# Rotary embedding of the retention heads: by a copy within SBUF and GpSimd, instead of by TensorE and VectorE

## What is computed

```python
def rotary(x, pos):
    ...
    x1, x2 = xf[..., :half], xf[..., half:]
    return jnp.concatenate([x1 * cos - x2 * sin, x2 * cos + x1 * sin], axis=-1)

def retention_mixer(cols, norm_w, pos):
    q, k, v, g = jnp.split(cols, 4, axis=-1)
    o = retention_chunkwise(rotary(q), rotary(k), v)     # scores * decay, times v
    mu = jnp.mean(o, axis=-1, keepdims=True)
    var = jnp.mean(jnp.square(o - mu), axis=-1, keepdims=True)
    o = (o - mu) * lax.rsqrt(var + NORM_EPS) * norm_w
    return jax.nn.silu(g) * o

def hybrid_layer(x, ...):
    proj = rms_norm(x, attn_norm_w) @ w_in
    mixed = jnp.concatenate([retention_mixer(ret_cols), dsa_mixer(dsa_cols), dilated_mixer(dil_cols)], axis=-1)
    x = x + mixed @ w_out
    h = rms_norm(x, mlp_norm_w)
    return x + jnp.square(jax.nn.relu(h @ w_up)) @ w_down
```

## Time and profile before

| | |
|---|---|
| time, median of 3 runs | 2440.71 us (2439.87 to 2441.47) |
| the profiled execution: its own time | 2440.98 us |
| its span in the profile | 2439.1 us |
| TensorE busy | 2382.6 us (98% of the span) |
| weight load of TensorE | 1905.6 us (78%) |
| VectorE busy | 1041.8 us (43%) |
| ScalarE busy | 955.3 us (39%) |
| GpSimd busy | 1026.4 us (42%) |

### The profile page before, as it was taken

One profiled execution on the slowest core, in us unless ns is written; L12 is line 12 of the kernel. 1 busy time (PEld: TensorE's weight loads), 2 busy tenths in 40 slices (PEclk: granted clock), 3 DMA queues, 4 the chain that ended last, 5 costly groups with the idle time before them and its releaser, 6 DMA issues.

```text
span 2439.1 us, 29458 instructions
## 1 busy us (share of the span) xinstructions
PE 2382.6 (98%) x11848; PEld 1905.6 (78%) x11848; DVE 1041.8 (43%) x1922; ACT 955.3 (39%) x1329; POOL 1026.4 (42%) x815
## 2 busy tenths in 40 slices
PE   8999999999999989999999989999999999999997
PEld 6777588888877767888888768888889769788887
DVE  4677641121337766211225545422224768322224
ACT  5344452232443445422335355421224485422223
POOL 4433144444444232444444453434444335444442
PEclk9999999999999999999999999999999999999999
DMA  4212123232232121323323212223323313322331
GB/s 162 79 52 96 34 88 104 88 103 87 83 108 86 36 95 35 104 87 103 104 87 117 87 35 70 83 90 104 104 85 106 104 37 102 104 87 87 104 104 52
DMA packets 138279, 212.36 MB, mean 87 GB/s; under 512 B 7456, under 2 KB 65952, under 8 KB 137888
## 3 DMA queue, kind: packets, MB, share of 16 engines
q1 hardware_dynamic: 138144, 210.48, 26.4%
HBM read 208.36 MB, written 2.10 MB: 86 GB/s over the span
## 4 chain that ended last, share of the span: by engine, by line
PE 54%; DVE 4%; ACT 4%; issue 1%; POOL 1%; ACTq 0%; DVEq 0%
PE ps L312 48%; PE ps L337 2%; POOL w_lo L275 1%; PE ps L1826 1%; DVE h_lo L569 1%; PE ps L845 1%; DVE x L692 1%; ACT w_hi L266 1%; PE ps L868 1%; PE ps L826 1%; DVE tmp_both L687 1%; ACT L493 0%; ACT h_hi L561 0%; PE ps L1298 0%; ACT r L1918 0%
## 5 line engine op out<-in xcount | busy, mean ns | idle before, releaser
L275 POOL TENSOR_TENSOR w_lo<-raw,w_hi 128x512 fp32r<-128x512 f32 (+1 forms) x776 | 992.7, 1312 | 1370.5 <-ACT w_hi L266 1370.2
L312 PE MATMUL ps<-h_hi,w_hi 128*128 128x512 f32 x1696 | 682.5, 402 | 14.2 <-POOL w_lo L275 13.8
L312 PE MATMUL ps<-h_hi,w_lo 128*128 128x512 f32 x1696 | 663.3, 391 | 0.0
L312 PE MATMUL ps<-h_lo,w_hi 128*128 128x512 f32 x1696 | 662.7, 391 | 0.0
L266 ACT ACTIVATE w_hi<-raw 128x2048 fp32r<-128x2048 f32 (+2 forms) x196 | 361.4, 1854 | 578.4 <-PE ps L312 457.6
L312 PE MATMUL ps<-hid_hi,w_hi 128*128 128x512 f32 x992 | 391.3, 394 | 4.8 <-DVE hid_lo L939 3.9
L312 PEld LDWEIGHTS ps<-h_hi,w_hi 128*128 128x128 f32 x1696 | 318.5, 188 | 98.0 <-issue 18.2
L312 PE MATMUL ps<-hid_hi,w_lo 128*128 128x512 f32 x992 | 388.1, 391 | 0.0
L312 PE MATMUL ps<-hid_lo,w_hi 128*128 128x512 f32 x992 | 387.9, 391 | 0.0
L312 PEld LDWEIGHTS ps<-h_lo,w_hi 128*128 128x128 f32 x1696 | 318.3, 188 | 69.9 <-issue 5.2
L312 PEld LDWEIGHTS ps<-h_hi,w_lo 128*128 128x128 f32 x1696 | 317.8, 187 | 70.4 <-issue 0.2
(11 more groups left out here) (304 smaller groups left out, 2775.6 us busy)
## 6 DMA issues: line engine op xcount, KB each, us to landing
raw<-in_w_up SPq DMA_DIRECT2D x32, 1024.0 KB, 5.5
raw<-in_w_down SPq DMA_DIRECT2D x32, 1024.0 KB, 5.0
raw<-in_ffn_w_gate SPq DMA_DIRECT2D x44, 512.0 KB, 3.9
raw<-in_ffn_w_up SPq DMA_DIRECT2D x44, 512.0 KB, 4.9
raw<-in_w_in SPq DMA_DIRECT2D x20, 1024.0 KB, 4.9
raw<-in_ffn_w_down SPq DMA_DIRECT2D x20, 1024.0 KB, 5.0
raw<-in_w_out SPq DMA_DIRECT2D x8, 1024.0 KB, 5.0
raw<-in_ev_w_in SPq DMA_DIRECT2D x8, 1024.0 KB, 5.3
```

Of the source, the lines that this page charges most:

```text
L275: pool.tensor_tensor(w_lo[slot.buf][:, k, 0:slot.width], raw[r][:, k, 0:slot.width], w_hi[slot.buf][:, k, 0:slot.width].bitcast(F32), ALU. ...
L312: mm = pe.matmul(o, lh, rh, start=first and q == 0, stop=last and q == 2, skip_group_check=True)
```

## The change

The matrix `rot_m` goes. SP copies the four blocks of `retqk` within SBUF with the halves of each head exchanged (8 transfers of 32 partitions by 4 KB, into the places of dilated queries that are no longer needed). POOL multiplies the copies with signed sines (4 instructions), after the next slot's low half multiplies q and k with the cosines (4) and adds (4), each 128x512. The tables of cosines and sines are loaded early, the decays alone later. With the rotation done beside the dilated attention, `RET` moves from step 6 to 4 and `GN` from 15 to 13; Ln and Exp stay at step 16 (`LN`). `out_b` is cut in two paces, 8 tiles in steps 12 to 17 (`out_b0`) and 8 in steps 18 to 22 (`out_b1`); the second waits for `gn_rstd`, the Exp of the group norm. The SiLU goes behind the last step of the dilated attention, and three top-k rounds go to steps 5, 7 and 17 of it.

```diff
             def _(sp):
...
+                load_slots(sp, s0 + 14)
+                sp.wait_ge(*at("s_ready", 8))
+                sg["rot_in"].by(sp.dma_start(cos_t[:], a["rtab"][:, T_COS:T_COS + S]), 16)
+                sg["rot_in"].by(sp.dma_start(sin_t[:], a["rtab"][:, T_SIN:T_SIN + S]), 16)
+                load_slots(sp, pl.s_mix + 1)
+                sp.wait_ge(*at("s_ready", 24))
+                sp.wait_ge(sems["bank_free"], BANKS + HALF * (pl.retqk + 1))
+                for i in range(2):
+                    for r in range(0, P, HD // 2):
+                        o = r ^ (HD // 2)
+                        sg["ret_swap"].by(sp.dma_start(swap[i][r:r + HD // 2, :, :],
+                                                       retqk[o:o + HD // 2, 2 * i:2 * i + 2, :]), 16)
                 load_slots(sp, pl.s_mix + 2)
                 sp.wait_ge(sems["bank_ready"], HALF * (pl.retv + 1))
-                sg["consts"].by(sp.dma_start(rtab[:], a["rtab"]), 16)
+                sg["decay_in"].by(sp.dma_start(decay[:], a["rtab"][:, T_DECAY:]), 16)
...
             def _(pool):
-                stream_lo(pool, pl.s_mix + 2)
-                pool.wait_ge(*at("consts", 16 * 3))
-                pool.wait_ge(sems["bank_free"], BANKS + HALF * (pl.retqk + 1))
+                stream_lo(pool, pl.s_mix)
+                pool.wait_ge(*at("rot_in", 32))
+                pool.wait_ge(*at("ret_swap", 16 * 8))
                 for j in range(4):
-                    sg["ret_cos"].by(pool.tensor_tensor(st_b[j][:], retqk[:, j, :], rtab[:, T_COS:T_COS + S], ALU.mult))
+                    o = swap[j // 2][:, j % 2, :]
+                    sg["ret_sin"].by(pool.tensor_tensor(o, o, sin_t[:], ALU.mult))
+                stream_lo(pool, pl.s_mix + 1)
+                for j in range(4):
+                    sg["ret_cos"].by(pool.tensor_tensor(retqk[:, j, :], retqk[:, j, :], cos_t[:], ALU.mult))
+                for j in range(4):
+                    pool.wait_ge(*at("ret_sin", j + 1))
+                    pool.wait_ge(*at("ret_cos", j + 1))
+                    sg["ret_rotd"].by(pool.tensor_tensor(retqk[:, j, :], swap[j // 2][:, j % 2, :], retqk[:, j, :],
+                                                         ALU.add))
                 stream_lo(pool, nxt.s0)
...
-            out_a, out_b = Pace(16, 0, 3), Pace(16, 16, 7)
-            ROT, RET, GN = 4, 6, 15
+            out_a, out_b0, out_b1 = Pace(16, 0, 3), Pace(8, 12, 6), Pace(8, 18, 5)
+            RET, GN, LN = 4, 13, 16
...
-                    if i == ROT:
+                    if i == RET:
                         pe.wait_ge(sems["bank_free"], BANKS + HALF * (pl.out_a + 1))
-                    if ROT <= i < ROT + 2:
-                        for j in (2 * (i - ROT), 2 * (i - ROT) + 1):
-                            sg["ret_rot"].by(pe.matmul(ps[:, 4 + j, :], rot_m, retqk[:, j, :], start=True, stop=True))
-                    if i == RET:
                         pe.wait_ge(*at("ret_rotd", 4))
...
-                    if i == out_b.step_of(9):
+                    out_b0.emit(i, tiles_b)
+                    if i == out_b1.first:
                         pe.wait_ge(*at("gn_rstd", 2))
-                    out_b.emit(i, tiles_b)
+                    out_b1.emit(i, tiles_b)
...
-                    if i == len(dil.units) + 1:
-                        act.wait_ge(sems["bank_free"], BANKS + HALF * (pl.dsaq + 1))
-                        alink(act, act.activation(gate[:], gate[:], ACT.Silu))
                 dil.scalar(act, beside_dil)
+                act.wait_ge(sems["bank_free"], BANKS + HALF * (pl.dsaq + 1))
+                alink(act, act.activation(gate[:], gate[:], ACT.Silu))
                 stream_hi(act, s0 + 18)
...
-                        take(1)
+                        take(2 if i in (5, 7, 17) else 1)
...
-                    if ROT <= i < ROT + 2:
-                        for j in (2 * (i - ROT), 2 * (i - ROT) + 1):
-                            dve.wait_ge(*at("ret_rot", j + 1))
-                            link(dve, dve.tensor_tensor(gn[j % 2][:], ps[:, 4 + j, :], rtab[:, T_SIN:T_SIN + S], ALU.mult))
-                            dve.wait_ge(*at("ret_cos", j + 1))
-                            sg["ret_rotd"].by(dve.tensor_tensor(retqk[:, j, :], gn[j % 2][:], st_b[j][:], ALU.add))
-                            dve.wait_ge(*at("ret_rotd", j + 1))
```

More of the change, by code:

```diff
@@ L37 @@
 HALF = 4
-T_IDENT, T_ONES, T_MEAN, T_ROT, T_LOGC, T_CAUSAL, T_POOL = 0, 128, 256, 384, 512, 1024, 1536
-T_SHARED = 1600
+T_IDENT, T_ONES, T_MEAN, T_LOGC, T_CAUSAL, T_POOL = 0, 128, 256, 384, 896, 1408
+T_SHARED = 1472
 T_COS, T_SIN, T_DECAY = 0, 512, 1024
@@ L58, in shape_tables @@
     t[:, T_MEAN:T_MEAN + P] = half / HD
[L60 to L64, removed]
     dist = q - (np.arange(S)[None] - (S - P))
@@ L77, in shape_tables @@
     r[:, T_COS:T_COS + S] = np.cos(ang.astype(np.float64))
-    r[:, T_SIN:T_SIN + S] = np.sin(ang.astype(np.float64))
+    sign = np.where(np.arange(P) % HD < HD // 2, -1.0, 1.0)[:, None]
+    r[:, T_SIN:T_SIN + S] = np.sin(ang.astype(np.float64)) * sign
     diff = np.arange(S)[None] - q
@@ L162, in build @@
         mean_m = tab[:, T_MEAN:T_MEAN + P]
-        rot_m = tab[:, T_ROT:T_ROT + P]
         p_t = [place(f"p{i}", [P, S], where=t_off[n]) for i, n in enumerate(("sq0", "sq1", "ssum", "p_more"))]
@@ L1149, in build @@
         rl = p_t
-        rtab = place("rtab", [P, T_RET], where=t_off["h_hi"])
+        decay = place("decay", [P, RET_H * S], where=t_off["h_hi"])
+        cos_t = place("cos_t", [P, S], where=t_off["dil_q_hi"])
+        sin_t = place("sin_t", [P, S], where=t_off["dil_q_lo"])
+        swap = [place(f"swap{i}", [P, 2, S], where=t_off[n] + 2048) for i, n in enumerate(("dil_q_hi", "dil_q_lo"))]
         st_b = [place(f"ret_st{i}", [P, S], where=t_off["h_lo"] + i * 2048) for i in range(4)]
@@ L1312, in retention @@
                             pe.wait_ge(*at("gn_in", j + 1))
-                            sg["gn_mean"].by(pe.matmul(ps[:, 4 + j, :], mean_m, gn[j][:], start=True, stop=True))
+                            sg["gn_mean"].by(pe.matmul(ps[:, 6 + j, :], mean_m, gn[j][:], start=True, stop=True))
                         if i == GN + 1:
@@ L1417, in retention @@
                             sg["gn_sq"].by(act.activation(st_b[j][:], gn[j][:], ACT.Square))
-                        if i == GN + 1:
+                        if i == LN:
                             act.wait_ge(*at("gn_var", j + 1))
@@ L1421, in retention @@
                     for j in range(2):
-                        if i == GN + 1:
+                        if i == LN:
                             sg["gn_rstd"].by(act.activation(st_b[j][:], st_b[j][:], ACT.Exp, scale=-0.5))
-                        if i == GN + 2:
+                        if i == LN + 1:
                             act.wait_ge(*at("gn_out", j + 1))
@@ L1591, in retention @@
                             add_out(pl.out_a, m, m)
[L1592 to L1600 removed]
+                    if i == RET:
+                        dve.wait_ge(*at("decay_in", 16))
                     for u in (2 * (i - RET), 2 * (i - RET) + 1):
@@ L1608, in retention @@
                             sg["ret_p"].by(dve.tensor_tensor(st_b[u % 4][:, 0:w], ps[:, 4 + u % 2, 0:w],
-                                                             rtab[:, T_DECAY + h * S:T_DECAY + h * S + w], ALU.mult))
+                                                             decay[:, h * S:h * S + w], ALU.mult))
                     if i == GN - 1:
@@ L1617, in retention @@
                             dve.wait_ge(*at("gn_mean", j + 1))
-                            sg["gn_c"].by(dve.tensor_tensor(gn[j][:], gn[j][:], ps[:, 4 + j, :], ALU.subtract))
-                    if i == GN + 1:
+                            sg["gn_c"].by(dve.tensor_tensor(gn[j][:], gn[j][:], ps[:, 6 + j, :], ALU.subtract))
+                    if i == LN:
                         for j in range(2):
```

2 lines of the change are left out of this document (1 added, 1 removed).

## The result

The changed kernel takes 2445.32 us (median of 20 runs, 2441.03 to 2447.0) against 2441.11 for the kernel before (20 runs, 2439.59 to 2443.75): ratio 1.0014, 95% interval 1.0008 to 1.0021. That is 4.2 us slower, inside the 0.2% that I called no change, and 4.1 above my 2441.2. The interval leaves out 1, so the kernel is slower, if by little, where my sum had +0.5. The profiled execution has 2445.91, its span is 2444.1 against 2439.1. The 20 executions of the changed kernel differ by up to 6 us, much as their mean granted clock does: the three at 0.995 took 2441.0 to 2442.4 us, the three at 0.991 took 2445.9 to 2446.7. The question is which terms of the sum held.

What follows compares the result with a forecast made beforehand. TensorE, busy 98% of the span, bounds the kernel. Terms sum to -0.5 us a layer, -1.0 for two, +0.5 with the first layer's clock: 2441.5 against the profiled 2440.98, as median 2441.2 us; range 2432.0 to 2446.5.

Steps and rivals of the forecast that it cites:

- Rotation's matmuls and waits: TensorE's rotation matmuls and the waits around them, before retention's scores, go: -3.7 and -2.8 us a layer.
- the spell behind them: Low clock after the rotation's waits, 4 us at 0.57 of full speed, goes: -1.7 us a layer.
- the waits at steps 4 and 5: TensorE waits for retention's first two decays, now at these steps: +0.7 us a layer, bounds 0 and 1.5.
- GpSimd's sums ahead of step 4: The rotation's sums end by 230.7 us, step 4 is at 240: 9 us early, costed at nothing.
- The rival of a late rotation: Copies take over 19 us instead of 7, then each microsecond costs twice: at 25 us, 2453; chance 0.02.
- Late waits: Late steps: TensorE waits 3.0 us for gn_rstd and 1.6 for rb, against 2.4 before: +2.3 us a layer.
- The end of the dilated attention: Masks and hid_lo on VectorE each wait for a GpSimd instruction, delaying TensorE: +3.9 us a layer, bounds -0.4 and +4.6.
- The faster rival: VectorE isn't held up at the dilated attention's end: -0.4 replaces 3.9, first layer's clock spell goes, 2431.1 us; chance 0.25.
- The clock at the front: Low clock after TensorE's longer pause for hid_lo: +1.5 us in the first layer, nothing in the second; bounds 0 and 1.7.
- The clock late in the layer: Low clock brought by the two late pauses, for Exp and rb: +0.8 us a layer, bounds 0 and 1.7.
- The slower rival: Clock stays low longer around the late pauses of 3.0 and 1.6 us and the one of 5.8: 2447.0; chance 0.13.

Runs made afterwards that it cites:

- e9: The changed kernel with each of its three mask instructions cut into two over half the columns: 2450.61 us, ratio 1.0037.
- e1: The changed kernel, but GpSimd waits for the dilated attention's last hid_lo before its cosines and sums: 2431.79 us, ratio 0.996.
- e10: e1 with each of the three mask instructions cut into two over half the columns: 2432.95 us, ratio 0.9963.
- e4: The changed kernel with five matmuls of no use on TensorE in its pause before out_a: 2441.4 us, ratio 0.9997.

## Why the prediction came out as it did

The mechanisms were right and the clock was undersized. That the time stayed within 0.2% says little by itself, for 0.2% is 4.9 us and the kernel lost 4.2 of them where the sum had 0.5. Point by point, a layer:

- **Rotation's matmuls and waits (-3.7, -2.8), and the spell behind them (-1.7): right.** From step 4's scores to the transposes of `rb` the changed kernel takes 246.48 to 289.22, 42.74 us, before it was 239.93 to 285.43, 45.50. That part holds these three, the waits at steps 4 and 5 (0.5 measured, 0.7 forecast) and the late waits, and my terms, with 2.1 us for the three tiles that moved ahead of the transposes, gave it 42.4. What each of the terms came to by itself this does not show.
- **GpSimd's sums ahead of step 4: right.** The last ends at 230.96; step 4 came at 246. The rival of a late rotation is excluded: the copies landed by 206.88, and took far less than the 19 us that it needed.
- **Late waits: right.** 3.1 us for Exp (forecast 3.0), 1.3 for `rb` in the second layer (1.6), and none shown in the first, where the tiles ran at half clock instead.
- **The end of the dilated attention (+3.9): right.** 5.66 us of wait against 1.9, +3.7, and e9 shows that the reason was too: each instruction waits its turn. The whole-instruction rule of the Trainium skill ("SBUF — State Buffer", "Who interferes with whom") would have given +4.6 by my estimate; the trace lies below it, since own work and wait together fill one turn (1.15 to 1.35 us for each half in e9, with 0.22 to 0.28 of own work in it). The faster rival, that VectorE is not held up, is out; e1 shows what it would have been worth, 2431.8, where I had worked out 2431.1.
- **The clock at the front (+1.5 in the first layer, 0 in the second): undersized.** From the end of step 0's scores to those of step 2 the first layer takes 16.2 us (225.90 to 242.12) against 9.65, +6.6. Of these 3.7 are the wait, so 2.8 are clock. In the second, 15.3 (879.83 to 895.10) against 11.1 (876.77 to 887.85), +4.2, so 0.5 is clock beyond the spell of 1.4 us that the kernel before has there. I had priced a pause of 5.8 us with the spell that follows one of 1.9 to 2.2.
- **The clock late in the layer (+0.8): undersized.** From the transposes of `rb` to the next `w_hi` it takes 7.43 us (289.22 to 296.65) and 8.57 (942.20 to 950.77). Before it was 8.16 with three tiles more, of 0.69 each, so without a spell 6.1 are due (e1's second layer has 6.12): 1.3 and 2.5.

Together the clock's terms were 1.5 + 2 x 0.8 = 3.1 and came out at 2.8 + 0.5 + 1.3 + 2.5 = 7.1. That is 4.0 us of the 4.5 by which the spans were missed (+5.0 where I had +0.5); the middle part adds 0.7 and the front gives back 0.4. The median was missed by 4.1. All this is read from one execution, at a clock of 0.991; the three executions at 0.995 came within 1.2 us of the forecast. The slower rival, 2447.0, described this: it named the pause of 5.8 and the two late ones as the places. Its condition, a low stretch that reaches past the transposes of `rb`, was met in both layers. I gave it 0.13; the result lies between it and the forecast, nearer to it.

## What to carry to other kernels

Work given to GpSimd is free only where VectorE has nothing short and urgent beside it: count VectorE's instructions there, not their bytes, and of the kinds that wait here (below) add about one GpSimd instruction's length for each that is on the path. A wait inserted on the offloaded engine (one line, 13.5 us) or an order that puts the urgent instruction first (12.1 us) gives the benefit of the change back. And when a pause of the busiest engine grows, price the low clock behind it by how long it lasts past the pause, in tiles, rather than by the last spell that was seen.

## What the runs showed that I had not expected

- **Not every VectorE instruction waits.** `key` (from PSUM and SBUF) takes 0.69 us and `retv` (from PSUM) 0.48 while GpSimd is busy, as without it. The masks and `hid_lo` wait every time. All four read and write SBUF alone, but that is not enough: the top-k rounds do too, and never wait. In the kernel before:

```profile
L1548 DVE MATCH_REPLACE8 sc<-top,sc x96: 406/543/679, 111.2 to 875.4; 128x256 f32<-128x256 f32 x32, 128x384 f32<-128x384 f32 x32, 128x512 f32<-128x512 f32 x32
```

  The longest of the 96 is no more than what 512 columns need; one at 219.22, amid a low half (218.06 to 220.58), takes 0.68 as does one at 224.60 with GpSimd idle. What sets the masks apart is their speed: 128 columns more cost them 0.06 us (e10), a top-k round 0.14. The copy `rb<-stat` is as fast (512 columns in 0.43) and is held up too, 0.69 at 220.15 in the changed kernel, amid a low half. This fits the section of the Trainium skill named above: it has instructions with two SBUF inputs wait, which is `hid_lo`, and those in a two-port mode, which it says copies and TENSOR_SCALAR can enter; that the masks were in such a mode no row says, it is inferred from their speed. Instructions of one column (`stat`, 0.15 us at 231.97, amid a low half) pass.
- **The pause of TensorE and the clock behind it have no fixed proportion.** A pause of 5.7 us lost 5.1 us of clock in the first layer and 3.4 in the second, the same late pause of 3.1 us lost 3.4 in one layer of e1 and nothing in the other. In time such a spell of the changed kernel costs between 1.3 and 2.8 us (fronts 2.8 and 1.9, late 1.3 and 2.5). Five matmuls of no use in the pause (e4) took the front's away in both layers.
- **Small transfers within SBUF are cheap.** The list of DMA issues of the changed kernel has

```profile
swap<-retqk SPq DMA_DIRECT2D x16, 128.0 KB, 2.3
```

  so each copy of 128 KB lands in 2.3 us, and a layer's eight are issued in 5.03 us (200.00 to 205.03), which is what sets when the sines can start.
